# Sample attention moved inside the prompt attention's stage of a hybrid decoder layer

## The reference, cut to what matters

```
def _dilated_attn_sample(q, k, v, k_buf, v_buf):
    k_all = concatenate([k_buf, k]);  v_all = concatenate([v_buf, v])
    for window, dilation in ((128, 1), (512, 4), (2048, 16)):
        idx = n_buf + arange(t)[:, None] - dilation * arange(window // dilation + 1)[None, :]
        kg, vg = k_all[:, idx], v_all[:, idx]
        sc = einsum('bthd,btjhd->bthj', q, kg) * dh ** -0.5
        lse = logsumexp(sc);  p = exp(sc - lse)
        outs.append(einsum('bthj,btjhd->bthd', p, vg))
```

## Time and the profile before

| what | us |
|---|---|
| median of 3 runs | 3780.71 |
| lowest and highest of them | 3777.63, 3788.79 |
| the profiled execution | 3789.74 |
| its span in the profile | 3788.0 |

### The profile page before, as it was taken

How to read it: one execution, slowest core, us unless ns; L and a number is a source line. 1 busy time by engine, 2 the same in 40 slices (tenths; PEclk the granted TensorE clock), 3 DMA queues, 4 the chain that set the end, 5 groups by cost and what they waited for, 6 DMA issues and landing times. The chain is left out here.

```text
span 3788.0 us, 75688 instructions
## 1 busy us (share of the span) xinstructions
PE 3176.1 (84%) x31060; PEld 2163.7 (57%) x31061; DVE 1419.9 (37%) x3319; ACT 1015.5 (27%) x2160; POOL 188.8 (5%) x311
## 2 busy tenths in 40 slices
PE   6999999999698888889982427996899999999930
PEld 4666777667488888778870103553455555555510
DVE  3445544342144334244447645665111111111135
ACT  4333444432122222266560003331111111111112
POOL 0000000000000000000000000000001000001011
PEclk9999999998799999999995668997899999999965
DMA  6111111113623223252246535540878776776755
GB/s 205 52 57 67 62 64 58 50 46 66 151 93 126 92 104 112 95 149 74 63 122 248 190 106 171 190 134 27 294 253 288 247 267 230 252 251 244 246 183 199
DMA packets 302881, 561.23 MB, mean 148 GB/s; under 512 B 98866, under 2 KB 123314, under 8 KB 295972
## 3 DMA queue, kind: packets, MB, share of 16 engines
q1 hardware_dynamic: 265380, 458.49, 35.9%
q0 software_dynamic: 20784, 73.15, 5.2%
q10 hardware_dynamic: 16464, 25.91, 2.1%
HBM read 408.98 MB, written 148.50 MB: 147 GB/s over the span
## 5 line engine op out<-in xcount | busy, mean ns | idle before, releaser
L294 PE MATMUL proj_main_ps<-proj_xt,proj_w 128*128 128x257 f32 (+1 forms) x1728 | 391.2, 382 | 0.0
L294 PEld LDWEIGHTS proj_main_ps<-proj_xt,proj_w 128*128 128x128 f32 x1728 | 328.8, 204 | 41.3
L2305 PE MATMUL moe_gate<-moe_w,moe_xt 128*64 128x256 f32 x2624 | 300.1, 382 | 6.7 <-DMA moe_w<-in_expert_w_dram 6.0
L2321 PE MATMUL moe_y_ps<-moe_w,moe_ht 128*64 128x512 f32 x1312 | 301.3, 601 | 3.1 <-ACT moe_ht L2360 3.1
L2305 PE MATMUL moe_up<-moe_w,moe_xt 128*64 128x256 f32 x2624 | 301.2, 382 | 0.0
L2305 PEld LDWEIGHTS moe_gate<-moe_w,moe_xt 128*64 128x64 f32 x2624 | 189.6, 138 | 137.4 <-issue 48.2
L317 PE MATMUL proj_main_ps<-proj_w,proj_xt 128*128 128x512 f32 (+1 forms) x560 | 247.5, 595 | 0.0
L2058 PE MATMUL out_proj_ps<-out_w,out_ct 128*128 128x512 f32 x544 | 241.0, 596 | 0.0
L2305 PEld LDWEIGHTS moe_up<-moe_w,moe_xt 128*64 128x64 f32 x2624 | 180.3, 137 | 97.5 <-issue 13.5
L1438 DVE CUSTOM_DVE_ANT_0 att_sc<-att_s_ps,att_mask 128x256 f32<-128x256 f32 (+1 forms) x384 | 117.5, 362 | 196.9 <-PE att_s_ps L1338 194.9
L1148 DVE COPY_PREDICATED rwkv_t<-rwkv_cons,rwkv_level_ps 128x512 f32<-128x512 uint32 (+1 forms) x168 | 109.3, 660 | 189.7 <-PE rwkv_level_ps L866 189.5
(11 more groups left out here) (332 smaller groups left out, 5184.2 us busy)
## 6 DMA issues: line engine op xcount, KB each, us to landing
moe_w<-in_expert_w_dram SPq DMA_DIRECT2D x96, 2048.0 KB, 10.0
y_rows<-rwkv_zero POOLq DMA_DIRECT2D x65, 512.0 KB, 4.8
y_rows<-moe_y ACTq DMA_DIRECT2D x164, 128.0 KB, 6.0
ft_p<-proj_uf SPq DMA_DIRECT2D x32, 642.0 KB, 3.3
rwkv_feat<-ft_p SPq DMA_DIRECT2D x16, 1284.0 KB, 7.0
satt_k<-in_cache_att_k_dram SPq DMA_DIRECT2D x16, 1024.0 KB
satt_v<-in_cache_att_v_dram SPq DMA_DIRECT2D x16, 1024.0 KB
o_p<-att_o SPq DMA_DIRECT2D x48, 260.0 KB, 2.1
```

Source lines behind the costliest of these rows:

```text
L294: last = mm(out[:, 0:w + 1], W[:, k, kind * C + m * P:kind * C + (m + 1) * P], XT[n % 2][:, k, 0:w + 1], start=(k == 0), stop=(k == KT - 1))
L2305: last = mm(bank[j * HB:(j + 1) * HB, 0:HF], XT[:, q, r * HB:(r + 1) * HB], W[:, k, j * HF:(j + 1) * HF], start=(k == 0), stop=(k == KT - ...
L2321: last = mm(py[j * HB:(j + 1) * HB, :], HT[:, c, r * HB:(r + 1) * HB], W2[s][:, k, j * 512:(j + 1) * 512], start=(k == 0), stop=(k == FE / ...
```

## The change

The two attention stages become one, `attention`. The sample's work is put into the steps of the prompt's units by a small table: sequence b has its turn around unit `at(b) = 13 + 8 b`, so around units 13, 21, and so on to 69.

- POOL takes over the products of keys and q (`product`, three for a sequence of 128 x 2048, `PRD` in two buffers), the product with the new keys (one for all 8 sequences) and the spreading by tile (`by_tile`, 128 x 864).
- DVE keeps the sums over heads (`head_sums`, 128 x 2048, after `p_copy` of units at(b) - 6, - 5 and - 3), masks, copies out of PSUM, maxima and `own_heads`.
- PE gets `turn_scores`, `turn_back` and `weigh_sample` at the end of steps at(b), at(b) + 4 and at(b) + 6, in the bank `t_ps[1]` that the prompt's transposes use. So it first waits for `p_high`, DVE's copy out of that bank, at the end of every odd step, and the next `turn_p` waits until DVE has read the sample's result out of it.
- ACT gets one exponential a sequence, after `o_copy`.
- SP gets all loads and stores of the sample, between those of the prompt. The keys wait until POOL has read their buffer, the values until PE has. `NV` goes from 6 to 5, and loads of q 1 to 3 move into the first three blocks.
- Maxima (`ML`) and weighted values (`OS`) have two buffers each; keys, values and scores have one.
- `clear_semaphores` now also stands between the RWKV stage and the attention.

```diff
+    NV, NX, NO, NSC = 5, 3, 3, 3
+    at_new, first_at, period = 7, 13, 8
+    at = lambda b: first_at + period * b
...
# SP, in the loop over blocks n, behind load_x(n + 3) and load_v(n + 2)
+                if n == 0:
+                    for b in range(B):
+                        rows = qkv_s[b * T:(b + 1) * T, 0:C]
+                        sp.dma_start(PRD[0][b * T:(b + 1) * T], ...).then_inc(sn_ld, 16)
+                    sp.dma_start(KNA, qkv_s[:, C:2 * C]).then_inc(sn_ld, 16)
+                    sp.dma_start(MS[:], masks_s).then_inc(s_in, 16)
+                    load_sample_q(0)
+                    load_sample_k(0, 0)
+                if 1 <= n < 4:
+                    load_q(n)
+                if 1 <= n < 3:
+                    load_sample_k(0, n)
+                if n == 4:
+                    load_sample_v(0)
+                for b in range(B):
+                    if n == (at(b) - 7) // 2 and b + 1 < B:
+                        if b >= 1:
+                            sp.wait_ge(s_prod, 3 * b)
+                        load_sample_q(b + 1)
+                        load_sample_k(b + 1, 0)
+                        load_sample_k(b + 1, 1)
+                    if n == (at(b) - 3) // 2 and b + 1 < B:
+                        load_sample_k(b + 1, 2)
+                    if n == (at(b) + 9) // 2:
+                        if b + 1 < B:
+                            load_sample_v(b + 1)
+                        store_sample(b)
                 if n >= 1:
                     store(n - 1)
...
# POOL
+            def product(b, g):
+                i = 3 * b + g
+                if g == 0:
+                    g_.wait_ge(sq_ld[b % 2], 16 * (b // 2) + 16)
+                g_.wait_ge(sk_ld[g], 16 * b + 16)
+                if i >= 2:
+                    g_.wait_ge(s_sum, i - 1)
...
+                nc.gpsimd.tensor_tensor(PRD[i % 2][:], keys, SQ[b % 2][:], ALU.mult).then_inc(s_prod, 1)
+            for b in range(B):
+                for j in range(3):
+                    product(b, j)
+                if b >= 1:
+                    by_tile(b - 1)
+            by_tile(B - 1)
...
# PE, in turn_p(u) and at the end of step u
+                    if u - 1 == at(b):
+                        pe.wait_ge(s_scores, b + 1)
+                    if u - 1 == at(b) + 4:
+                        pe.wait_ge(s_probs, b + 1)
+                    if u - 1 == at(b) + 6:
+                        pe.wait_ge(s_own, b + 1)
...
+            def weigh_sample(b):
+                pe.wait_ge(sv_ld, 64 * b + 64)
+                pe.wait_ge(s_lm, b + 1)
+                for i in range(NT):
+                    mm(t_ps[1][0:NQ, :], LM[:, i, :], SV[:, i, :], start=(i == 0), stop=False, ...)
+                mm(t_ps[1][0:NQ, :], PN[:], VN[:], start=False, stop=True, ...).then_inc(s_weighted, 1)
+            def sample(u):
+                pe.wait_ge(p_high, u + 1)
...
+                if u % 2 == 1:
+                    sample(u)
...
# DVE, behind mask_min(u + 2) and p_copy(u)
+                    for g in range(3):
+                        if u == at(b) - (6, 5, 3)[g]:
+                            head_sums(b, g)
+                    if u == at(b) - 1:
+                        mask_scores(b)
+                    if u == at(b):
+                        maxima(b)
+                    if u == at(b) + 4:
+                        copy_probs(b)
+                    if u == at(b) + 6:
+                        own_heads(b)
...
-    prompt_attention(nc, qt_p, kc_p, vc_p, ident, consts["band"], o_p, m_p)
-    sample_attention(nc, qkv_s, a["cache_att_k"], a["cache_att_v"], ident, consts["sample"], o_s, m_s)
+    clear_semaphores(nc)
+    attention(nc, qt_p, kc_p, vc_p, qkv_s, a["cache_att_k"], a["cache_att_v"], ident, consts["band"], consts["sample"], o_p, m_p, o_s, m_s)
     clear_semaphores(nc)
```

More of the change, by code:

```diff
@@ L1218, with attention @@
 VW = DH + 1
-def prompt_attention(nc, qt, k_in, v_in, ident_in, mask_in, o_out, m_out):
+T = 4
+NQ = 3 * T * H
+NT = 9
+def attention(nc, qt, k_in, v_in, qkv_s, cache_k, cache_v, ident_in, mask_in, masks_s, o_out, m_out, os_out, ms_out):
     S = k_in.shape[0]
@@ L1291, in _ @@
             load_v(1)
-            for j in range(1, 4):
-                load_q(j)
             for n in range(NBK):
@@ L1303, in _ @@
                 sp.wait_ge(o_st[j], 32 * len(range(j, NBK, NO)))
+            for j in range(2):
+                sp.wait_ge(s_st[j], 96 * (B // 2))
         @blk.gpsimd
@@ L1309, in _, with by_tile @@
             last.then_inc(ones_set, 1)
+            wide = lambda x, p: x.rearrange("p (o k) -> p o k", o=1).broadcast_to([p, T, C])
+            def product(b, g):
[5 more added lines that the diff above has]
+                    g_.wait_ge(s_sum, i - 1)
+                elif i == 0:
+                    g_.wait_ge(s_new, 1)
+                else:
+                    g_.wait_ge(s_new_sum, 1)
+                keys = wide(SK[:, 0, :], P) if g == 0 else SK[:, key_group(g), :]
+                nc.gpsimd.tensor_tensor(PRD[i % 2][:], keys, SQ[b % 2][:], ALU.mult).then_inc(s_prod, 1)
+            def by_tile(b):
+                g_.wait_ge(s_probs, b + 1)
+                if b >= 1:
+                    g_.wait_ge(s_weighted, b)
+                else:
+                    g_.wait_ge(s_new, 1)
+                nc.gpsimd.tensor_tensor(LM[:], PB[:].rearrange("p (o q) -> p o q", o=1).broadcast_to([P, NT, NQ]), tile_of, ALU.mult).then_inc(s_lm, 1)
+            g_ = g
+            g.wait_ge(ones_set, 1)
+            g.wait_ge(sn_ld, 16 * (B + 1))
+            nc.gpsimd.tensor_tensor(PRD[1][0:B * T], wide(KNA, B * T), PRD[0][0:B * T], ALU.mult).then_inc(s_new, 1)
+            g.wait_ge(s_in, 16)
+            for b in range(B):
+                for j in range(3):
+                    product(b, j)
+                if b >= 1:
+                    by_tile(b - 1)
+            by_tile(B - 1)
         @blk.tensor
@@ L1346, in turn_p @@
                     pe.wait_ge(p_high, u)
+                if u - 1 == at_new:
+                    pe.wait_ge(s_new_copied, 1)
+                for b in range(B):
+                    if u - 1 == at(b):
[4 more added lines that the diff above has]
+                        pe.wait_ge(s_own, b + 1)
                 for hl in range(4):
@@ L1424, in _ @@
                     k_copy(u // 2 + 2)
+                for b in range(B):
+                    if u == at(b):
+                        sample_exp(b)
         @blk.vector
@@ new lines, in copy_new, with head_sums, mask_scores @@
+            def copy_new():
+                v.wait_ge(s_new_turned, 1)
+                v.tensor_copy(SNT[:], t_ps[1][0:NQ, 0:B * T]).then_inc(s_new_copied, 1)
+            def head_sums(b, g):
+                v.wait_ge(s_prod, 3 * b + g + 1)
+                if b >= 1:
+                    v.wait_ge(s_turned, b)
+                v.tensor_reduce(SS[:, 32 * g:32 * g + 32], PRD[(3 * b + g) % 2][:].rearrange("p t (h k) -> p (t h) k", h=H), AX.X, ALU.add).then_inc(s_sum, 1)
+            def mask_scores(b):
+                v.wait_ge(s_sum, 3 * b + 3)
+                v.scalar_tensor_tensor(SS[:], SS[:], DH ** -0.5, buf_mask, ALU.mult, ALU.add).then_inc(s_masked, 1)
@@ new lines, in copy_probs, with own_heads @@
+            def copy_probs(b):
+                v.wait_ge(s_back, b + 1)
+                if b >= 1:
+                    v.wait_ge(s_weighted, b)
+                v.tensor_copy(PB[:], t_ps[1][:, 0:NQ])
+                v.tensor_copy(PN[:], t_ps[1][0:T, NQ:2 * NQ]).then_inc(s_probs, 1)
+            def own_heads(b):
+                v.wait_ge(s_weighted, b + 1)
+                v.tensor_tensor(OM[:], t_ps[1][0:NQ, :], diag, ALU.mult).then_inc(s_own, 1)
+                v.wait_ge(s_own, b + 1)
+                v.tensor_reduce(OS[b % 2][:, 0:DH], OM[:].rearrange("p (h k) -> p k h", h=H), AX.X, ALU.add).then_inc(s_o, 1)
@@ new lines, in sample @@
+            def sample(u):
+                if u == at_new - 2:
+                    sum_new()
+                if u == at_new - 1:
+                    mask_new()
+                if u == at_new:
+                    copy_new()
+                for b in range(B):
+                    for g in range(3):
+                        if u == at(b) - (6, 5, 3)[g]:
+                            head_sums(b, g)
+                    if u == at(b) - 1:
+                        mask_scores(b)
+                    if u == at(b):
+                        maxima(b)
+                    if u == at(b) + 4:
+                        copy_probs(b)
+                    if u == at(b) + 6:
+                        own_heads(b)
@@ L1473, in sample_masks @@
     buf = np.where((c[None] > 0) | (i >= t[None]), 0.0, NEG)
-    new = np.where(np.where(c[None] > 0, i == t[None], i <= t[None]), 0.0, NEG)
+    j = i % T
+    new = np.where(np.where(c[None] > 0, j == t[None], j <= t[None]), 0.0, NEG)
     tile = np.where(c == 0, 0, T * (c - 1) + 1 + t)
```

225 lines of the change are left out of this document (89 added, 136 removed).

## The result

The changed kernel took 3682.49 us, the median of 4 runs (3679.29 to 3696.63), against 3779.17 us of the kernel before on the same chip: a ratio of 0.9747, interval 0.9716 to 0.9778. The forecast was 3606 us, a gain of 175 us; the gain was 97 us, and the time lies above the range's 3655. Faster was right, the size was not, and the question is where 78 us went.

A forecast was written before the change was run, and what follows sets the result against it. PE bounds the prompt attention; in the sample attention PE and DVE take turns. Removing 269.9 us and putting back 79 + 10.6 + 1.6 + 1 + 2.9 = 95 saves 175 us: 3780.7 becomes 3606 us, range 3582 to 3655.

The forecast's parts named there:

- What SP gets: SP's queue in the merged stage: stores wanted after 7.6 us land after 2.1; the new clear ahead adds 2.9 us.
- The sum: Whole change: 95 us put back against 269.9 taken away, worth 175 us, giving 3606 us.
- A store or a load is late in SP's one queue: Rival, merged stage: stores miss their 7.6 us by 2.1 at 24 places, 50 us, 3656 us; 9 in 100.
- the clock's fall: Rival, merged stage: PE falls off the full clock; slower than before at a mean of 0.71; 2 in 100.
- PE's products: Merged stage: ten products a sequence take 8.99 us at the full clock, 71.9 us for 8 sequences.
- transposes: PE in the merged stage: 0.9 us a sequence with pipe fills, 7 us for 8 sequences.
- POOL's product: POOL in the merged stage: 4.2 us for 2048 elements, costing nothing up to 5.5 us a product.
- waits for DVE: PE in the merged stage: 10.6 us behind DVE's late copies, plus 1.6 us for `p_high` in short odd steps.
- ACT's 1 us: Merged stage: one exponential a sequence delays `exps(u + 2)`; felt only where `turn_x` waits for ACT's copy, 1 us.
- the + 2.9 for a clear: Seam ahead of the merged stage: 5.14 us with `clear_semaphores`, against 2.28 and 1.89 without.
- The lower end of the forecast's case: Case 3580 to 3640 (77 in 100); lower end from 3585: no waits, products at 8.9 us a sequence.
- The rival of POOL and DVE: Merged stage: POOL and DVE get in each other's way, 64 us of PE's time, 3670 us; 8 in 100.

The follow-up runs named there:

- e6: The changed kernel with four output buffers (o_p, m_p) of the prompt instead of three: 3576.23 us, 0.9494 of the kernel before.
- e1: The changed kernel with the prompt's stores moved to ScalarE's DMA queue: 3663.05 us, 0.9714 of the kernel before.
- c: The changed kernel itself, measured again on the chip of other runs: 3665.6 us, 0.9726 of the kernel before.
- e2: The changed kernel with the sample's values loaded one block later: 3645.52 us, 0.9684 of the kernel before.
- e5: The changed kernel with the sample's loads spread, at most 2 MB in a block: 3628.42 us, 0.9619 of the kernel before.
- e8: e3 with the sample's six small stores on ScalarE's queue, two in each of three steps: 3626.62 us, 0.9619 of the kernel before.
- e3: The changed kernel without the sample's loads of sequences 1 to 7: 3615.31 us, 0.9568 of the kernel before.
- e4: The changed kernel with only the sample's six small stores moved to ScalarE's queue: 3662.30 us, 0.9723 of the kernel before.

## Why the prediction was wrong

**The step that failed is "What SP gets"**: "The store of a block's `O` and `NM` is wanted two steps later (7.6 us) and lands after 2.1 us." The 2.1 us was the median of a stage without the sample's traffic, used for a kernel that issues 4.5 MB ahead of a store; there the median of `o_p` is still 2.1, but the landing of an `m_p` took up to 14.7 us. I walked one sequence and set SP's order against its waits, but did not lay two sequences side by side, where the values of one and the keys of another fall on one block. The sum has no term for it at all. It measured 68.0 us of DVE's waits, and with the clock some 98 us of the stage.

How the loss splits, over the whole stage from its first load to the next stage's first load, in the changed kernel and in e6:

```profile
1603.83:2149.13 545.30, 478.84 (x2817) 371.04 (x2817) 249.87 (x963) 232.32 (x609) 129.51 (x38) 0.82 0.52 151
1595.26:2043.00 447.74, 428.15 (x2817) 326.07 (x2817) 247.16 (x963) 231.26 (x609) 129.74 (x38) 0.98 0.61 184
```

The same 2817 instructions of PE take 98 us more: 47 of them are idle time (66.5 against 19.6 us), 51 are PE's work at a lower clock. By windows of 1 us, nine of the falls in the changed kernel came behind a wait and three did not; those three have an estimated sixth of the time at 0.50, weighted by PE's busy time.

**The rival with the right cause had the wrong price.** "A store or a load is late in SP's one queue" gave 24 x 2.1 = 50 us and 3656. The places were fewer (11) and the misses longer (up to 11.6 us), and that the idle time of PE, 47, came near the price is luck. What the rival left out was the clock, another 51. Its chance of 9 in 100 leaned on "the DMA engines would be busy for 254 of 450 us only", 0.56. That share was right (0.54) and no argument: a mean says nothing of a burst, where it stood at 1.03. And by e1 the one queue was not what made the store late.

**The clock.** I let PE's own busy share argue for the full clock, and kept the clock's fall as a rival of its own, at 2 in 100. Here most of it is the second half of another rival. In the windows above one idle stretch of 11 us brings 0.50, and 1.00 is back some 5 us after PE starts again (1748.6); after the next wait (DVE's ended at 1799.30) it was back at 1814 only. Near the stage's end 1.6 us of idle time preceded a fall that lasted to the end of the short units. The idle time does not give the clock's share. Against e6's stage, in the profiled executions:

| run | more idle time of PE, us | more busy time of PE, us |
|---|---|---|
| changed kernel | 47 | 51 |
| c | 37 | 45 |
| e2 | 25 | 33 |
| e5 | 12 | 41 |
| e8 | 6 | 39 |
| e3 | 3 | 24 |

**What was right**, checked on e6, where almost nothing is late. e6's 0.9494 of 3780.7 is 3589 us, 17 below the forecast. The forecast put back 95 us; e6's stage and seams put back 81: from the first load to the end of the last issue 632.3 us became 444.6, and the seams ahead and behind are 1.0 us shorter in sum, so 189 us are gone, and 81 of the 269.9 are put back (in the forecast 175 and 95).
- PE's products: 63.4 + 8.8 = 72.2 us for 8 sequences (71.9), transposes 6.7 (7).
- POOL's product 4.54 us, below the 5.5 from which it would have been late. The Trainium skill, GPSIMD Engine Reference, section 3.1, has 4497 ns: the trace agrees within 1%.
- The forecast's waits for DVE were 10.6 + 1.6 us, and PE waited some 3 for DVE's copies in e6; ACT's 1 us was nothing that shows. These terms, with the + 2.9 for a clear, are the 14 us by which the sum was too high: the seam ahead of the stage grew by 0.9 us and the one behind it, which had a clear already, shrank by 2.0, so 5.14 was not the price of a clear. The error hid behind the larger one. The lower end of the forecast's case took 8.9 us a sequence for "the products at their columns", where the bound of 68 us gives 8.5. SP's queue at the two seams of e6:

```profile
1591.39 0.66 SPq L819 DMA_DIRECT2D out_dram<-rwkv_sv  x1
1595.26 0.34 SPq L1290 DMA_DIRECT2D att_x<-out_dram  x1
...
2039.40 0.43 SPq L1307 DMA_DIRECT2D m_p<-att_nm  x1
2043.00 0.32 SPq L1811 DMA_DIRECT2D out_y<-yr_p  x1
```

- The rival of POOL and DVE falls for the dense work (2276 ns a sum, 245 ns for `mask_scores`). It is true in one instruction that I had not thought of, the mask of the new keys' scores, which has two SBUF inputs and stands beside POOL's second product. POOL and DVE in the changed kernel:

```profile
1643.17 4.53 POOL L1406 TENSOR_TENSOR att_s_prd<-att_s_k,att_s_q 128x2048 f32<-128x2048 f32 x1 [11.70 <-DVE att_s_sn L1624]
1644.93 2.88 DVE L1629 SCALAR_TENSOR_TENSOR att_s_snm<-att_s_sn,att_s_masks 32x96 f32<-32x96 f32 x1
```

It ended at 1647.81, POOL's at 1647.70; the same kind of operation took 0.247 us in the kernel before. The Trainium skill, SBUF — State Buffer, section "SBUF: two separate sides", says that a vector instruction with two SBUF inputs and a GpSimd one that reads SBUF lock each other out, and the later one waits. This trace agrees, with 2.88 us against 0.247. It happens once here, for 2.6 us, and PE shows no wait for it.

## What to carry to other kernels

When loads are moved beside a stage that stores, don't price the store by its old landing time. List what each step of a queue issues, with all the units in flight side by side, take the largest burst of bytes ahead of a store, and set that landing time against the time until its buffer is reused. If it doesn't hold, one more output buffer is the cheapest cure: here one number was worth 2.3% (0.9726 to 0.9494), more than any reordering of loads or queues, and nothing at all in the kernel without the burst (1.0004). And the idle time of PE is not the whole price of a wait: work at the lower clock cost as much again here, and several times as much in e3, e5 and e8, where the waits were short.

## What the runs showed of the hardware that was not expected

Small stores have late landings beside them on another queue too. e3 and e8, both without loads, differ in the queue of the sample's small stores and in their steps (six together in e3, two in each of three steps in e8). In e8, 17 of the prompt's `m_p` were issued from 1.5 us before to 4.5 us after a small store on ScalarE's queue. They landed 3.1 to 6.6 us after their issue; the median of the other 31 was 1.9. The median of all is 3.0 in e8 and 1.9 in e3. The other queue is not what raises it: in e4, with all six together on ScalarE's queue, it is 2.4, against 3.0 in the changed kernel. What fits all three is the number of the prompt's stores that have small stores beside them; no run tests that alone. The median of `m_s` itself was 2.6 in e3 and 5.4 in e8.

PE's clock fell in several profiles with no wait of PE just before, 2 to 3 us behind 9 us of products that PE's records show as fully busy, and where no wait followed it stayed at 0.50 for 3 to 34 us with PE busy all the time. Behind a wait near the stage's end it stayed at 0.50 until the stage was over, some 50 us, in short units. Other executions of nearly the same code have none of this.
